# Squares of x1 summed by token with single-column products, in a one-core Trainium2 kernel

## What is computed

```python
y = hybrid_mixer(h, ...)                                  # ends in out @ w_o
x = x + g_a[:, None, :] * rms_norm(y, attn_post_norm)     # this x is x1
h = modulate(rms_norm(x, ffn_pre_norm), sh_f, sc_f)       # h * (1 + scale) + shift
y = conv_geglu_ffn(h, w_up, conv_w, conv_b, w_down)
```

## Time and profile before

| | |
|---|---|
| median of 3 runs | 1762.83 us (1761.37 to 1764.17) |
| the profiled execution | 1761.64 us |
| its span, first to last instruction | 1759.8 us |
| PE busy | 1696.8 us, 96% of the span |
| DVE busy | 1251.7 us, 71% |
| ACT busy | 892.1 us, 51% |
| POOL busy | 19.7 us, 1% |
| DMA | 377.10 MB, mean 214 GB/s |

### The profile page before, as it was taken

One profiled execution on the slowest core, in us unless ns is written; L12 is line 12 of the kernel. 1 busy time (PEld: TensorE's weight loads), 2 busy tenths in 40 slices (PEclk: granted clock), 3 DMA queues, 4 the chain that ended last, 5 costly groups with the idle time before them and its releaser, 6 DMA issues.

```text
span 1759.8 us, 33243 instructions
## 1 busy us (share of the span) xinstructions
PE 1696.8 (96%) x13841; PEld 1654.6 (94%) x13841; DVE 1251.7 (71%) x1877; ACT 892.1 (51%) x1445; POOL 19.7 (1%) x31
## 2 busy tenths in 40 slices
PE   2899999999999999999999999999999999999997
PEld 2799999999999999999999999999899999999997
DVE  6888899898787667667667656656865576665655
ACT  8545445555565445445445435535734544446554
POOL 0000010000000000000000000000000000000000
PEclk7899999999999999999999999999999999999999
DMA  9899787688647666667667666565355444764341
GB/s 366 337 359 375 253 296 287 243 296 328 259 159 231 209 205 227 214 204 229 209 193 232 217 187 183 180 189 183 109 169 168 144 133 132 225 209 130 111 128 63
DMA packets 89285, 377.10 MB, mean 214 GB/s; under 512 B 10032, under 2 KB 10416, under 8 KB 76592
## 3 DMA queue, kind: packets, MB, share of 16 engines
q1 hardware_dynamic: 89136, 374.98, 62.7%
HBM read 372.84 MB, written 2.10 MB: 213 GB/s over the span
## 4 chain that ended last, share of the span: by engine, by line
PE 89%; DVE 5%; DMA 3%; issue 1%; ACT 1%; DVEq 0%; SPq 0%; ACTq 0%
PE ps L609 26%; PE ps L610 25%; PE ps L611 25%; PE ps L730 4%; DMA raw<-in_ada 3%; DVE raw L1577 2%; PE ps L764 1%; PE ps L749 1%; PE ps L772 1%; DVE w_lo L1568 1%; PE ps L714 1%; PE ps L992 0%; PE ps L994 0%; PE ps L993 0%; PE ps L638 0%
## 5 line engine op out<-in xcount | busy, mean ns | idle before, releaser
L609 PE MATMUL ps<-h_hi,w_hi 128*128 128x256 f32 x3248 | 938.4, 289 | 8.3 <-DVE h_lo L1641 5.2
L610 PE MATMUL ps<-h_lo,w_hi 128*128 128x256 f32 x3248 | 920.4, 283 | 0.0
L611 PE MATMUL ps<-h_hi,w_lo 128*128 128x256 f32 x3248 | 920.2, 283 | 0.0
L1568 DVE TENSOR_TENSOR w_lo<-raw,w_hi 128x1024 fp32r<-128x1024 f32 x510 | 622.7, 1223 | 262.7 <-ACT w_hi L1138 261.7
L1138 ACT ACTIVATE w_hi<-raw 128x1024 fp32r<-128x1024 f32 x510 | 538.6, 1058 | 511.5 <-PE ps L611 466.5
L609 PEld LDWEIGHTS ps<-h_hi,w_hi 128*128 128x128 f32 x3248 | 624.2, 192 | 16.7 <-issue 11.5
L610 PEld LDWEIGHTS ps<-h_lo,w_hi 128*128 128x128 f32 x3248 | 624.7, 192 | 1.2
L611 PEld LDWEIGHTS ps<-h_hi,w_lo 128*128 128x128 f32 x3248 | 624.4, 192 | 0.0
L1577 DVE SCALAR_TENSOR_TENSOR raw<-raw,c_wide 128x2048 f32<-128x2048 f32 x96 | 219.3, 2287 | 18.3 <-DMA raw<-in_ada 17.4
L609 PE MATMUL ps<-g_hi,w_hi 128*128 128x256 f32 x704 | 199.3, 283 | 0.6 <-DVE conv L1975 0.6
L610 PE MATMUL ps<-g_lo,w_hi 128*128 128x256 f32 x704 | 199.2, 283 | 0.0
(11 more groups left out here) (237 smaller groups left out, 1208.6 us busy)
## 6 DMA issues: line engine op xcount, KB each, us to landing
raw<-in_weights SPq DMA_DIRECT2D x510, 512.0 KB, 3.8
raw<-in_ada SPq DMA_DIRECT2D x96, 1024.0 KB, 6.0
x<-in_x SPq DMA_DIRECT2D x1, 2048.0 KB, 12.7
out_y<-x SPq DMA_DIRECT2D x3, 512.0 KB, 2.9
c_wide<-in_c_wide SPq DMA_DIRECT2D x1, 1024.0 KB, 5.4
consts<-in_consts SPq DMA_DIRECT2D x1, 798.0 KB, 8.9
out_y<-x SPq DMA_DIRECT2D x2, 256.0 KB, 2.6
params<-in_params SPq DMA_DIRECT2D x1, 504.0 KB, 7.4
```

The lines of the kernel that those rows point to most:

```text
L609: nc.tensor.matmul(out, wh, hi[:, k, :], start=start, stop=False)
L610: nc.tensor.matmul(out, wh, lo[:, k, :], start=False, stop=False)
L611: last = nc.tensor.matmul(out, wl, hi[:, k, :], start=False, stop=stop)
L1568: V.tensor_tensor(w_lo[:, h % W_SLOTS, :], raw[:, raw_slot("w", h), :], w_hi[:, h % W_SLOTS, :].bitcast(F32), ALU.subtract).then_inc(lo_dv ...
```

## The change

x1 goes the way of the token sums. `token_square` sums the squares of all 16 tiles in place in the columns 0 and 1 of x1's bank, two f32 products of one moving column for each tile; ACT's root and DVE's reciprocal work on 128x2; `widen` spreads the result into bank 6, and line 1652 of `modulate` reads it there, from PSUM, where it read rstd from SBUF. The filling products are set anew: 6 for 10 before y1 is spread, 5 also behind the fourth group, 6 before and 10 after the spreading of x1 for the 24.

```diff
--- before.py
+++ after.py
@@ -312,7 +312,7 @@
         delta3 = sb("delta3", [P, 3, 4 * HEADS], BF16)
         negsink = sb("negsink", [P, 16])
         sub_r = sb("sub_r", [P, 16])
-        token_r = sb("token_r", [P, 6, 2])
+        token_r = sb("token_r", [P, 7, 2])
         sq_acc = sb("sq_acc", [P, S])
         table_out = sb("table_out", [P, 1])
         eps_col = sb("eps_col", [P, 1])
@@ -531,14 +531,14 @@
         CHUNKS_1 = [(0, 2), (2, 4), (4, 8), (8, 12), (12, 14), (14, 16)]
         CHUNKS_2 = [(0, 1), (1, 2)] + [(k, k + 2) for k in range(2, KT, 2)]
         SCALED = dict(y1=0, y2=len(CHUNKS_1))
-        TOKEN = dict(q=0, kv=1, y1=2, y2=3, x3=4, x0=5)
-        WIDE_AT = dict(x0=1, q=2, kv=3, y1=4, y2=5, x3=6)
+        TOKEN = dict(q=0, kv=1, y1=2, y2=3, x3=4, x0=5, x1=6)
+        WIDE_AT = dict(x0=1, q=2, kv=3, y1=4, x1=5, y2=6, x3=7)
         TOKEN_TILES = dict(x0=KT, q=4, kv=2, y1=KT, y2=KT, x3=KT)
         TOKEN_COLUMN = dict(x0=0, q=0, kv=8, y1=0, y2=0, x3=0)
-        WIDE_BANK = dict(x0=7, q=6, kv=6, y1=5, y2=2, x3=2)
-        WIDE_COLUMN = dict(x0=0, q=0, kv=S, y1=0, y2=0, x3=0)
+        WIDE_BANK = dict(x0=7, q=6, kv=6, y1=5, x1=6, y2=2, x3=2)
+        WIDE_COLUMN = dict(x0=0, q=0, kv=S, y1=0, x1=0, y2=0, x3=0)
         NORM = dict(x0=0, q=1, kv=2, y1=3, x1=4, y2=5, x2=6, x3=7)
-        FEATURES = dict(x0=D, q=512, kv=256, y1=D, y2=D, x3=D)
+        FEATURES = dict(x0=D, q=512, kv=256, y1=D, x1=D, y2=D, x3=D)
         HN = dict(x0=0, x1=16, x2=32)
         XN = dict(y1=0, y2=16, out=32)
 
@@ -652,6 +652,15 @@
                     last = nc.tensor.matmul(ps[:, NORM_BANK[stage], at:at + 1],
                                             squares_in(SQ[stage] + k)[:, a * P:a * P + P], mean_mat[:, 0:1],
                                             start=True, stop=True)
+                last.then_inc(sq_used, 1)
+
+            def token_square(stage, k):
+
+                pe.wait_ge(sq_ready, k + (SQ[stage] + 1))
+                for a in range(2):
+                    last = nc.tensor.matmul(ps[:, NORM_BANK[stage], a:a + 1],
+                                            squares_in(SQ[stage] + k)[:, a * P:a * P + P], mean_mat[:, 0:1],
+                                            start=k == 0 and a == 0, stop=k == KT - 1, skip_group_check=True)
                 last.then_inc(sq_used, 1)
 
             def token_totals(stage):
@@ -925,14 +934,17 @@
                 if j == KT - 1:
                     token_sums("y1", KT - 2)
             token_sums("y1", KT - 1)
-            keep_going(H_FF, 10)
+            keep_going(H_FF, 6)
             widen("y1")
             keep_going(H_FF, 20)
             for a, b in CHUNKS_1:
-                mean_square("x1", b, a, KT)
-                if b <= 8:
+                for k in range(a, b):
+                    token_square("x1", k)
+                if b <= 12:
                     keep_going(H_FF, 5)
-            keep_going(H_FF, 24)
+            keep_going(H_FF, 6)
+            widen("x1")
+            keep_going(H_FF, 10)
 
             def down_first(u, g0):
 
@@ -1161,7 +1173,7 @@
 
             def token_root(stage):
                 r = token_r[:, TOKEN[stage], :]
-                if stage in ("y2", "x3"):
+                if stage in ("x1", "y2", "x3"):
                     act.wait_ge(sq_used, SQ[stage] + KT)
                     total = ps[:, NORM_BANK[stage], 0:2]
                 else:
@@ -1378,7 +1390,7 @@
             nc.scalar.activation(masks_bf[:, :, :].rearrange("p a b -> p (a b)"), con("causal", 0, 2 * P), ACT.Copy
                                  ).then_inc(consts_cast, 1)
             squares("x1", KT, lambda k: x[:, k, :], (x_ready, lambda k: XN["y1"] + k + 1))
-            root("x1")
+            token_root("x1")
             act.wait_ge(mod_ready, N_SUMS[SH_F])
             h_high("x1", SH_F)
 
@@ -1959,7 +1971,7 @@
             dve.wait_ge(inputs_loaded[6], 16)
             residual("y1")
             lo(H_O_B + KT - 1 + 4)
-            invert("x1")
+            token_invert("x1")
             modulate("x1", lambda k: scale_cols[:, 2, k:k + 1], SH_F)
 
             dve.wait_ge(y_zero, 1)
```

## The result

The changed kernel takes 1766.70 us in the median of 15 runs (1764.29 to 1770.51), the kernel before 1762.83 (1758.95 to 1765.55, 15 runs): a ratio of 1.0025, 95% interval 1.0017 to 1.0033. It is slower by 3.9 us, between 3.0 and 5.8 by the interval. The profiled execution took 1766.03 us for 1761.64, 4.4 us more, with a span of 1764.1 for 1759.8.

What follows compares the result with a forecast made beforehand. TensorE was taken as the bound, 89% of the chain of waits. The steps summed to -0.34 us at the full clock; a clock fall during tiles 4 to 7 added +6.4, giving +6.0, about 1768 us, range 1761.0 to 1770.6.

Steps and rivals of the forecast that it cites:

- a fall of the clock within the sums: TensorE's clock drops from 2.4 to 1.2 GHz during the thin x1 sums, +6.0 us net; chance 0.48.
- Step 1: Fillers before y1's spreading cut from 10 to 6: the spreading and what follows start earlier, -0.32 us.
- Step 2: x1 sums as two one-column f32 products a tile: 0.42 us for 0.41, +0.1 over eight tiles.
- Step 3: Fourth group of 5 fillers, between tiles 11 and 12 of the x1 sums, not hidden: +0.78 us.
- Step 4: Smaller root on ACT and reciprocal on DVE, 128x2 instead of 128x256: -0.21 and -1.58 us.
- Step 5: Spreading x1's result by two 128-column products until DVE reads it, +0.82 us; six fillers ahead of it, +0.07.
- Step 6: Line 1652 on DVE reading PSUM instead of rstd costs nothing extra: 0 us.
- The sum at the full clock: All steps of the x1 stage added with the clock staying at 2.4 GHz: -0.34 us.
- The low clock's prices: At 1.2 GHz in the x1 stage: 0.42 us more a tile, 0.1 a filler, 0.6 for the spreading.
- The clock that holds: Rival: TensorE stays at 2.4 GHz through the x1 sums, 1762.5 us, no change that can be told; chance 0.34.
- PSUM reads: Rival: line 1652 pays more for PSUM than SBUF, about +0.7 us net, 1763.5 us; chance 0.03.
- the hidden reciprocal: Rival: the shorter reciprocal was already covered, so the fourth filler group leaves +0.8 us, 1763.6 us; chance 0.03.

Runs made afterwards that it cites:

- f_fillers_each_tile: The changed kernel with 2 fillers behind each tile of the x1 sums instead of 5 behind the groups: 1769.42 us, ratio 1.0039.
- c_y1_ten: The changed kernel with 10 fillers again instead of 6 before y1 is spread: 1769.87 us, ratio 1.0043.
- d: The changed kernel without the fourth group of 5 fillers in the x1 sums: 1766.61 us, ratio 1.0023.
- a_moving128: The changed kernel with the x1 sums' products moving all 128 columns of ones instead of one: 1762.16 us, ratio 1.0002.
- h_changed_again: The changed kernel run once more with no edit: 1766.57 us, ratio 1.0027.
- k_five_each_tile: The changed kernel with 5 fillers behind each tile of the x1 sums: 1767.56 us in a single run.
- b: The kernel before, wide sums kept, with 6 fillers instead of 10 before y1 is spread and a fourth group of 5: 1762.55 us, ratio 1.0005.

## Why the prediction was right

The forecast was a fall of the clock within the sums, 1768.0 us, with a range of its own of 1766.3 to 1770.6; measured were 1766.7 and the fall. The mechanism is what it had right. The number is weaker support: the fall had a chance of 0.48, and the whole range, from 1761.0 on, also took in no change. By its steps:

- **The bound.** That a moment in the stage reaches the end in full fits: 4.15 us in the stage, 4.3 in the span, and PE full behind it. It holds to about 2 us only, since what follows the stage takes 1271.1 to 1273.3 us in the twelve profiles. Nor does the stage of one profile stand for the median of its runs where the place of the fall moves: 9.0 us of stage for 6.6 us of time in f, 6.0 for 7.9 in c, 2.8 for 4.7 in d.
- **Step 1** (-0.32). The spreading of y1 came 1.42 us after the last sums for 1.75, so -0.33. But it ran at the low clock and DVE began 1.22 us after its start for 0.81, so the step brought +0.08. I had not expected a fall here. At the full clock it is worth -0.23, for with six fillers DVE begins 0.91 us after the spreading's start (a_moving128).
- **Step 2** (0.42 us a tile; one column wins nothing over 256). 0.43 with a_moving128, 0.45 in the changed kernel at the high clock.
- **Step 3** (+0.78). 485.34 - 484.66 = 0.68 in a_moving128; 1.21 at the low clock.
- **Step 4** (-0.21, -1.58). Root 0.26, reciprocal 0.17, as said.
- **Step 5** (0.80 from the spreading to DVE). 0.75 in a_moving128 (488.59 - 487.84); 1.09 at the low clock. There I had added 0.6, from the lengths of the entries; it was 0.3.
- **Step 6** (0 for PSUM). Line 1664 with ps has the same median as before, and the Trainium skill's dearer PSUM source (VectorE: DVE Perf Modes, the TRN2 errata) doesn't show:

```profile
L1664 DVE SCALAR_TENSOR_TENSOR probs<-x,scale_cols,ps x28: 472/476/489, 61.1 to 503.5; 128x256 f32<-128x256 f32 x28
```

- **The sum at the full clock** (-0.34 us). a_moving128 is that case: 16.90 - 17.38 = -0.48.
- **The low clock's prices.** The doubled one-column entries, a bound from the 128-column ones, came out at 0.82 us a tile for the 0.84 that I took. For a fall in tiles 4 to 7 I had +6.4 over the full clock; c_y1_ten, where it fell so, shows 6.45, or 6.2 without its four fillers more. For a fall at tile 8 I had +4.7 in all; the changed kernel, where it fell inside tile 8, shows 4.15, of which 0.31 came before the sums. Over a_moving128's rows: up to tile 4 +0.31; tiles 4 to 7 +0.01; eight tiles 6.22 us for 3.41, +2.81; fillers between them +0.53; six fillers 1.43 for 0.80, +0.63; spreading of x1 to DVE 1.09 for 0.75, +0.34; together 4.63, less 0.48, is 4.15. So like for like it was 3.8 for the 4.7: the tiles were put at 3.4, the spreading at 0.6.
- **The size.** The sum gave +6.0, the measured change is +3.9. The fall was put a few tiles too soon, and the low clock's prices were somewhat high. Line 1652 (now 1664) starts at 492.44, just short of the 493 to 495.5 that I gave. The 1768.0 lies between what the +6.0 gives from the profiled time (1767.6) and from the median (1768.8). The place of the fall moves between the profiles; how it moves over the 15 runs, of which one was profiled, is not known, and their spread of 6.2 us doesn't tell, since the kernel before spreads by 6.6.
- **The rows it argued from.** Both falls had idleness before them too: 1.09 us at 189, and 2.32 us ahead of the y2 sums, which I hadn't named. They could not tell thin products from waiting. The runs do: a_moving128 keeps its clock over a wait of 0.51 us, and in h_changed_again PE is busy for the whole of every slice from 475 to 482, with the fall at 481.9.
- **The rivals.** The clock that holds, PSUM reads, and the hidden reciprocal are out: the first by the slices, the second by line 1664, the third by a_moving128, whose fourth group is paid and whose stage is shorter all the same.

## What to carry to other kernels

Before a wide product is replaced by a narrow one, look at what sets its pace: where the weights change for every product, the narrow one was no faster here, and the width is then free to be kept for the clock. Read PEclk in slices of 1 us beside the starts of entries, and not the busy share, wherever TensorE's work is made thin, fillers taken out or a wait added. And measure a small stage by a distance within each run, since the runs as wholes scatter more than it is worth.

## What the runs showed that I had not expected

- The profile counted PE as busy for the whole of every slice at the low clock from 483 to 492. The Trainium skill (TensorE: Matmul & The Clock Gate, Part 1) has the gate follow how busy the engine has been; in this trace the profile's busy share doesn't tell it, since a_moving128 is no busier by that share and keeps 1.00.
- An f32 product of 128 moving columns costs the same as one of a single column when the stationary side changes each time: for tiles 4 to 7, 1.80 us with 128 (482.27 - 480.47 in a_moving128) and 1.81 with one (481.81 - 480.00 in the changed kernel at the high clock).
- With two fillers behind each tile the clock fell, with five it stayed (f_fillers_each_tile and k_five_each_tile, one profile each, which differ in PE's waits too).
- Six fillers behind y1's one-column sums were met by a fall in four profiles of nine. From the spreading's start to DVE it took 1.26, 1.22, 1.13 and 0.92 us there (b, the changed kernel, d, h), for 0.91 where the clock held, so it cost up to 0.35 us and in h nothing. Why it falls in some executions and not in others of like order stays open. A form of the sums in one pass, with the squares as f32r, was not tried.
